# Per-tile waits in the output products, the index key first, value tiles between head turns, and earlier copies of full modulation packs

## The reference

```python
h = rms_norm(x, norm1_g);  proj = h @ w_in       # q k v iq ik iw a c g
q, k = rope(rms_norm(q)), rope(rms_norm(k))      # 8 and 2 heads of 128
iq, ik = rope(iq), rope(ik);  iw = iw * const    # index: 8 query heads of 64, one key, one weight per head
score = sum_h iw[h] * relu(iq[h] @ ik.T)         # then the 64 best keys of each query
y_attn = masked_attention(q, k, v, top64(score)) @ w_attn_out
y_conf = silu(layer_norm(conv31(a_val * sigmoid(a_gate)))) @ w_conf_out
y_sc   = (c_b * conv3(c_c * c_x)) @ w_sc_out
x = x + (g0 * y_conf + g1 * y_attn + g2 * y_sc) @ w_o
x = x + (silu(u_gate) * u_val) @ w_down          # u = conv3(rms_norm(x) @ w_up)
```

## Time and profile before

| | before |
|---|---|
| median of 3 runs (lowest, highest) | 3490.5 us (3489.91, 3490.7) |
| profiled execution: own time | 3491.94 us |
| profiled execution: span from first to last instruction | 3490.1 us |
| PE busy | 3377.6 us, 97% |
| DVE busy / ACT busy | 1629.2 us, 47% / 567.9 us, 16% |
| mean granted clock of PE, share of 2.4 GHz | 0.984 |
| transfers | 440.70 MB, mean 126 GB/s |

### The profile page before, as it was taken

How to read it: one execution, slowest core, us unless ns; L and a number is a source line. 1 busy time by engine, 2 the same in 40 slices (tenths; PEclk the granted TensorE clock), 3 DMA queues, 4 the chain that set the end, 5 groups by cost and what they waited for, 6 DMA issues and landing times. The chain is left out here.

```text
span 3490.1 us, 41818 instructions
## 1 busy us (share of the span) xinstructions
PE 3377.6 (97%) x16652; PEld 2766.3 (79%) x16652; DVE 1629.2 (47%) x3362; ACT 567.9 (16%) x1197; POOL 23.6 (1%) x41
## 2 busy tenths in 40 slices
PE   8999999999999999999999998999999999998999
PEld 7787888887888888888886554788887888765888
DVE  4567223235673233166564564564556655455100
ACT  2121112111111122110002333100011000134100
POOL 0000000000000000000000010000000000001000
PEclk9999999999999999999999999999999999999999
DMA  5777547635867467423232220232322323222464
GB/s 180 217 195 240 181 150 212 171 119 151 230 207 228 157 187 199 121 73 109 67 103 56 67 49 25 73 103 67 88 89 66 109 73 94 59 91 37 134 165 112
DMA packets 655632, 440.70 MB, mean 126 GB/s; under 512 B 24336, under 2 KB 654512, under 8 KB 655312
## 3 DMA queue, kind: packets, MB, share of 16 engines
q1 hardware_dynamic: 652416, 430.28, 42.6%
q0 software_dynamic: 1552, 6.07, 1.1%
q10 hardware_dynamic: 1472, 1.68, 0.2%
HBM read 436.94 MB, written 1.05 MB: 125 GB/s over the span
## 5 line engine op out<-in xcount | busy, mean ns | idle before, releaser
L1815 PE MATMUL psum<-hh,ring 128*128 128x256 f32 (+2 forms) x5344 | 1264.3, 395 | 9.0 <-ACT hh L1174 4.8
L1815 PEld LDWEIGHTS psum<-hh,ring 128*128 128x128 f32 (+1 forms) x5344 | 1011.9, 191 | 236.4 <-issue 102.5
L1815 PE MATMUL psum<-arena,ring 128*128 128x256 f32 x1568 | 341.6, 381 | 8.2 <-DVE arena L1538 5.5
L1815 PEld LDWEIGHTS psum<-arena,ring 128*128 128x128 f32 x1568 | 298.9, 191 | 50.6 <-DVE arena L1538 6.3
L2007 PE MATMUL psum<-hh,arena 128*128 128x256 f32 x1056 | 254.6, 385 | 7.7 <-issue 5.2
L2007 PE MATMUL psum<-hh,ring 128*128 128x256 f32 x1056 | 247.6, 389 | 4.0 <-ACT hh L1174 4.0
L2007 PE MATMUL psum<-arena 128*128 128x256 f32 x1056 | 238.9, 379 | 0.0
L2007 PEld LDWEIGHTS psum<-hh,ring 128*128 128x128 f32 x1056 | 206.2, 196 | 34.7 <-issue 4.7
L1453 DVE SCALAR_TENSOR_TENSOR arena<-arena,par 128x255 f32<-128x255 f32 (+14 forms) x480 | 225.1, 469 | 17.0
L2007 PEld LDWEIGHTS psum<-hh,arena 128*128 128x128 f32 x1056 | 203.5, 193 | 36.9 <-issue 8.8
L2030 PE MATMUL psum<-arena 128*128 128x256 f32 x1056 | 231.8, 379 | 0.0
(11 more groups left out here) (258 smaller groups left out, 2817.7 us busy)
## 6 DMA issues: line engine op xcount, KB each, us to landing
ring<-in_ffn_w SPq DMA_DIRECT2D x176, 512.0 KB, 5.0
ring<-in_w_mod SPq DMA_DIRECT2D x72, 1024.0 KB, 7.5
ring<-in_w_in SPq DMA_DIRECT2D x54, 1024.0 KB, 5.2
ring<-in_w_up SPq DMA_DIRECT2D x88, 512.0 KB, 5.3
ring<-in_w_in SPq DMA_DIRECT2D x84, 512.0 KB, 5.2
ring<-in_w_down SPq DMA_DIRECT2D x16, 1408.0 KB, 6.9
ring<-in_ffn_w SPq DMA_DIRECT2D x12, 1536.0 KB, 6.6
ring<-in_ffn_w SPq DMA_DIRECT2D x12, 1280.0 KB, 5.8
```

The source lines that it names most:

```text
L1815: ins = mm(o[0:rows_, 0:T], w[:, k, c0:c0 + rows_], src[:, k, 0:T], start=(k == 0), stop=(k == kt - 1))
```

## The change

1. `conf_out` and `wo` no longer wait for the whole source before their first product: the eight products of their first output tile wait one by one for the tile that each reads.
2. The index key, tile 4, is projected first (`INDEX_ORDER`), the index weights right after the second tile, and each score product waits only for the key and for the tile with its own head. The chunk with the key comes ahead of the other two.
3. The two value tiles move up: one before the copy that turns the ninth head, one before that of the tenth.
4. ACT's copy of a pack gets a step of its own, `mod_m`, right behind the twelfth `mod` step of the pack (behind the last one for the third pack); PE's waits stay as they were.

```diff
--- before.py
+++ after.py
@@ -49,6 +49,7 @@
 SLOTS = 4
 GROUPS = ((0, 12), (12, 22))
 PROD = 7
+INDEX_ORDER = (4, 0, 1, 2, 3)
 ARENA = 25064
 SLOT = 3072
 
@@ -191,6 +192,8 @@
         p.step("mod", l, c)
         p.chunks.append(("mod", l, c))
         p.last_mod[("mod", l, c)] = len(p.last_mod) + 1
+        if c % PACK == PACK - 1 or c == NMOD * KT // 2 - 1:
+            p.step("mod_m", l, c // PACK)
     if c and c % PACK == 0 or c == NMOD * KT // 2:
         p.step("mod_t", l, (c - 1) // PACK)
         p.job("mod_t", l, (c - 1) // PACK)
@@ -220,24 +223,24 @@
         if 1 <= i < nqk + 1:
             p.step("qss", l, i - 1)
             p.job("qss", l, i - 1)
+        if i >= nqk:
+            p.step("v", l, i - nqk)
+            p.job("v", l, i - nqk, chunk=("v", l))
         if 2 <= i:
             p.step("qrot", l, i - 2)
             p.job("qrot", l, i - 2)
-        if i == nqk:
-            for t in range(TT):
-                p.step("v", l, t)
-                p.job("v", l, t, chunk=("v", l))
-    for i in range(6):
-        if i < 5:
-            p.step("iq", l, i)
-            p.job("iq", l, i, chunk=("iq", l, i // 2))
-        if i == 4:
+    for n in range(6):
+        if n < 5:
+            i = INDEX_ORDER[n]
+            p.step("iq", l, n, i)
+            p.job("iq", l, n, chunk=("iq", l, i // 2))
+        if n == 1:
             for t in range(TT):
                 p.step("iw", l, t)
                 p.job("iw", l, t, chunk=("iq", l, 2))
-        if i >= 1:
-            p.step("irot", l, i - 1)
-            p.job("irot", l, i - 1)
+        if n >= 1:
+            p.step("irot", l, n - 1, INDEX_ORDER[n - 1])
+            p.job("irot", l, n - 1)
     for t in range(TT):
         for h in range(IDX_HEADS):
             p.step("idx", l, t, h)
@@ -1141,7 +1144,7 @@
                     i = r[0]
                     evacuated(act, job[("up", l, i, 0)])
                     do(nc.scalar.activation(up_buf[:, i % 2, 0, :], up_buf[:, i % 2, 0, :], ACT.Silu), up_silu, FT * l + i + 1)
-                elif kind == "mod_t":
+                elif kind == "mod_m":
                     n = packs(l, r[0])
                     act.wait_ge(mod_taken, mod_count(l, r[0]))
                     if n >= 2:
@@ -1407,7 +1410,7 @@
                     free(ts(iw_s[:, r[0], :], bank(j)[:, 0:IDX_HEADS], IDX_HEADS ** -0.5 * IDX_DIM ** -0.5, None, ALU.mult), j)
                 elif kind == "irot":
                     i, j = r[0], job[("irot", l, r[0])]
-                    dst = iq_t[:, i, :]
+                    dst = iq_t[:, r[1], :]
                     evacuated(dve, job[("iq", l, i)])
                     do(tt(dst, iraw[:, i % 2, :], const("cos_i"), ALU.mult))
                     produced(dve, j)
@@ -1861,8 +1864,8 @@
                 elif kind == "v":
                     project_tok(job[("v", l, r[0])], arrived(("v", l)), 0, 256, r[0])
                 elif kind == "iq":
-                    i = r[0]
-                    project(job[("iq", l, i)], arrived(("iq", l, i // 2)), P * (i % 2), h, S)
+                    n, i = r
+                    project(job[("iq", l, n)], arrived(("iq", l, i // 2)), P * (i % 2), h, S)
                 elif kind == "iw":
                     project_tok(job[("iw", l, r[0])], arrived(("iq", l, 2)), P, IDX_HEADS, r[0])
                 elif kind == "irot":
@@ -1873,7 +1876,7 @@
                     t, hd = r
                     nk = P * (t + 1)
                     p0 = 64 * (hd % 2)
-                    pe.wait_ge(idx_roped, 5 * l + 5)
+                    pe.wait_ge(idx_roped, 5 * l + 2 + hd // 2)
                     done(mm(begin(job[("idx", l, t, hd)])[:, 0:nk], iq_t[p0:p0 + 64, hd // 2, t * P:(t + 1) * P],
                             iq_t[p0:p0 + 64, 4, 0:nk], start=True, stop=True))
                 elif kind == "a":
@@ -1924,12 +1927,10 @@
                         pe.wait_ge(sc_ready, KT * (l + 1))
                     elif kind == "att_out":
                         evacuated(pe, job[("att_o", l, HEADS - 1)])
-                    elif kind == "conf_out":
-                        pe.wait_ge(conf_ready, KT * (l + 1))
-                    else:
-                        pe.wait_ge(merged_ready, KT * (l + 1))
+                    tiles = {"conf_out": (conf_ready, KT * l, 1), "wo": (merged_ready, KT * l, 1)}
                     src = {"sc_out": scv, "att_out": attn, "conf_out": aconv, "wo": merged}[kind]
-                    project(job[(kind, l, i)], arrived((kind, l, i // 2)), P * (i % 2), src, S)
+                    project(job[(kind, l, i)], arrived((kind, l, i // 2)), P * (i % 2), src, S,
+                            ready=tiles.get(kind) if i == 0 else None)
                 elif kind == "up":
                     w = arrived(("up", l, r[0]))
                     for u in range(2):
```

## The result

The changed kernel takes 3470.8 us (median of 4 runs, 3468.5 to 3475.8) against 3490.6 us (4 runs, 3489.9 to 3493.3): a ratio of 0.9941, 95% interval 0.9928 to 0.9953. The forecast was 3474 us; the gain is 19.8 us where 16.0 were expected. The profiled execution took 3472.4 us, with a span of 3470.6.

What follows compares the result with a forecast made beforehand. PE, busy 97% of the span, was taken as the bound. Terms 8.5 - 1.1 + 6.5 + 2.1 = 16.0 us took the profiled 3491.94 to 3475.9; with the median 1.4 lower, 3474 us, 8-in-10 range 3464 to 3482.

Steps and rivals of the forecast that it cites:

- Heads: Value tiles before the ninth and tenth heads' turns: that stretch falls from 12.44 to 8.19 us a layer, 8.5 us gained.
- The lower bound of 5.0: Least gain at the head turns, 5.0 us, if the half-clock stretches come back elsewhere, each costing 1.7 us.
- Index part by order: Last index projection to first gate projection shortens to 10.7 us: gains of 1.7 and 2.4, 4.1 us for both layers.
- Index part by clock: Half clock behind the index weights, over dense projections, two stretches a layer: a loss of 2.6 us each, 5.2 in both.
- The edit as a whole: Index edit, order gain less clock loss: 4.1 - 5.2 = -1.1 us, ends +4.1 and -6.1.
- Packs: Earlier copy of full packs on ACT removes PE's modulation waits: 4.2 + 2.3 = 6.5 us gained, bounds 5.2 and 6.5.
- Waits by tile: First output tile of `wo` no longer waits for the late last merged tile: 2.1 us gained; `conf_out` gives nothing.
- The key's chunk: The index key's chunk comes two places earlier and still arrives in time: 0 us, late chance under 1 in 100.
- the one on waits by tile and packs: Rival: `wo` still waits for its last tile, packs give 5.2 us: gain 12.6, time 3478; chance 0.08.
- The kinder clock: Rival: no clock fall behind index weights, or two stretches vanish at `down` and in the second block: 3469 to 3466; chance 0.20.
- The dearer clock: Rival: three half-clock stretches a layer behind index weights, or half clock on the gate projections: 3477.5 to 3480; chance 0.20.
- the case in which the change is slower: Rival: removed waits are paid back in half-clock stretches on PE's dense work; 15 more give 3500 us; chance 0.02.

Runs made afterwards that it cites:

- e1: Only the value tiles moved between the head turns, against the kernel before: 3485.2 us, ratio 0.9983.
- e7: The full change, with the first output tile of `down` also waiting for its 22 source tiles one by one: 3463.3 us, 0.9920 of the kernel before.
- e10: The full change, with the index weight products streaming 136 columns instead of 8: 3469.9 us, 0.9939 of the kernel before.
- e11: The full change with index weights between the last two turned tiles, `down` waiting by tile, and index weight products of 136 columns: 3459.2 us, 0.9908 of before.
- a2: The full change measured again, nothing altered: 3471.0 us, 0.9943 of the kernel before.
- e5: The full change without its index edit: 3475.7 us, 0.9957 of the kernel before.
- e5b: The full change without its index edit, run again on one chip with a2: 3476.2 us, 0.9958 of the kernel before.
- e2: Only the index edit (key first, weights behind the second projection, scores waiting by pair of heads), against the kernel before: 3490.2 us, 0.9996.
- e3: Only the earlier copy of full packs, against the kernel before: 3486.2 us, 0.9990.
- e6: The full change, with the index weights between the last two turned tiles instead of behind the second projection: 3468.1 us, 0.9930 of the kernel before.
- e4: Only the waits by tile in the first output tile of `conf_out` and `wo`, against the kernel before: 3487.3 us, 0.9990.

## Why the prediction was near, step by step

- **Heads: 8.5 forecast, 8.3 in the stages.** Right in mechanism and size. By the medians of e1 it was 5.9; in its profiled execution part of the clock that was kept at the heads was lost in the feed-forward stage, most of it behind `down`. The lower bound of 5.0 named this.
- **Index part by order, 4.1: right.** 3.00 us to the first sum and 4.06 to the gate projection came out as worked out from DVE's queue. Layer 0 of e7 has the order of the change and no half clock: 29.20 us, where the kernel before took 31.69 and 30.99. That is 2.5 + 1.8 = 4.3 us for the order alone.
- **Index part by clock, -5.2: right in place, and in size by luck.** The half clock came behind the index weights, and e10 and e11 show that it goes when they are widened. Two stretches a layer were taken at 2.6 us, 0.9 for the one that lies half over the weights. Against the 29.20 us at full clock, one stretch costs 1.7 us (30.89) and two cost 3.3 (32.52 in both layers of a2): the first is paid in full, since the weights slow down as well (4.23 us instead of 3.63 in layer 1 of the change). The profiled execution had three stretches instead of four, 5.0 us in all, and the two errors cancelled. So the stage came to +0.75 us (-0.80 and +1.56) against +1.1; in a2, with four, to +2.4.
- **The edit as a whole, -1.1: the step that failed.** It summed this stage and let it stand for the kernel. Taken off the whole change (e5, e5b) the edit is worth some 5 us by the medians, and the mean granted clock is higher with it, 0.9863 against 0.9839. Alone (e2) it gained 0.9 us, with an interval from a loss of 1.7 to a gain of 4.5. What it does to the clock outside the rows of this stage stood at nothing in the sum. The traces do not place it, and why the clock is higher stays open.
- **Packs: 6.5 forecast, 7 in the stages.** 2.42 and 2.02 in attention; in the feed-forward part 1.20 in layer 1, where both kernels have one half-clock stretch behind `down`, and in layer 0 the same hidden behind a new one: 0.28 - 1.7 = -1.4. The exact sum is 7.0 us; the worry of 0.33 us left at each switch did not come true. By the medians of e3 it is 4.9.
- **Waits by tile: 2.1 forecast, 2.7 measured**; `conf_out` had nothing to give, and eight waits in a row cost PE nothing: `wo` follows it with no gap in its rows.
- **The key's chunk: 0, right.** No wait on `ring` stands in the index part.
- **What the sum did not hold:** 1.59 us at the start, which is no effect of the change (the tenth head's sums stand at 59.3 us in e5 and at 58.2 in e5b, the same kernel, and between 57.9 and 59.5 in all), and 2.45 us in the second block, whose instructions are the same. The four edits gave 8.3 - 0.75 + 7.0 + 2.7 = 17.2 us, the new stretch behind `down` took 1.7, and these two gave 4.0. These last 4.0 us are chance as far as the runs show: without them the profiled execution would have taken 3476.4 us, where 3475.9 was forecast for it. The other way round, the median lies 3.2 us under the forecast, less than the 7.5 us by which the second block alone differs between profiled executions. The half clock behind 1410 us, put at about 20 stretches, was some 24 in the kernel before (82 us by its trace, 3.4 each) and 23 after.

Of the rivals, the one on waits by tile and packs is refuted by their stages. The kinder clock (3469) and the forecast (3474) are about as near to the measured 3470.8, which lies between them; but the kinder clock's own condition, no fall behind the weights or fewer stretches at `down`, did not hold in the profiled execution, which had one more at `down`. The dearer clock (3477.5 to 3480) did not come: no layer had a third stretch, and the gate projections ran at full clock. Nor did the case in which the change is slower.

## What to carry to other kernels

Put work that needs nothing ahead of each step that waits for a normalisation or a turn, one piece to a step, and issue the copy of a full buffer where it fills, not where it is next read: both gave their waits in full in their own stages. Place narrow products where another engine sets the pace behind them (e6), not ahead of dense products (the change): the stage is 1.5 to 4.2 us shorter, though the whole of e6 is not told from the change. A stage's table tells what an edit does there, while the medians of 5 to 11 runs tell what it is worth: here the two differed by 1 to 6 us, and the mean granted clock of the whole is what the runs show beside that.

## What the hardware showed that was not expected

- The same wait of 2.18 us is followed by half clock for 3.4 us in the kernel before, and by none in layer 1 of e2 and e4: 1.7 us, by no edit near it.
- Products of 8 columns hold PE nearly as long as those of 136 (3.63 and 3.87 us for 32 records), but half clock follows the narrow ones in 23 of 24 profiled layers, and the wide ones in none of four.
- Half clock is free over the scores: the index part takes 28.4 us with it (e6, layer 1) and 28.6 with wide products (e11). Over the index weights and the turned tile ahead of the scores it is not (29.4 us, e6, layer 0).
- Taking away a wait of PE gave 0.27 to 0.3 us more than the row of the wait has, at the heads (2.18), at `wo` (1.07) and at `down` (2.73).
- The whole kernel is at half clock for some 104 us of 3471 in the profiled execution after the change, and 112 before (mean granted clocks 0.985 and 0.984). Between the runs with and without an edit in a part of 60 us this differs, by the mean clock, by 17; the second block alone has between 65 and 92 in the profiled executions.
